# The expert loop's first input slices are copied ahead of the combine weights, and the weights' transposes move into the loop's last turn

## Chip, core and metric

One NeuronCore of a Trainium2 chip runs one program. The metric is the device time of one execution in microseconds, from the hardware profiler; the kernel before was timed three times. The engines are named as in the profile: PE (matmuls; PEld is its weight load), DVE, ACT and POOL (vector, scalar and general work), SP (here it only issues DMAs, in order, and waits on semaphores between them).

## What is computed

One inference step of a decoder layer for a prompt group (272 tokens with the meta tokens) and a sample group (32 tokens), 304 tokens in all: a gated merge of two mixers, then a mixture of 32 experts, of which every token uses two, then a norm. The part that this change touches is the mixture. From the reference:

```python
combine = jnp.sum(jax.nn.one_hot(flat_idx, N_EXPERTS, dtype=jnp.float32) * ew[..., None], axis=1)
y = jnp.zeros_like(xf)
for e in range(N_EXPERTS):
    he = jax.nn.silu(xf @ w_exp_gate[e]) * (xf @ w_exp_up[e])
    y = y + combine[:, e:e + 1] * (he @ w_exp_down[e])
```

All is float32. An expert's weights are three matrices of 1024 x 256 numbers (gate, up, down), 1 MiB each; the 32 experts have 96 of them, 100.7 MB.

## The kernel before

The kernel is written engine by engine: each engine has its own instruction list, and semaphores alone set the order between them.

*Gather.* After the router each of the 608 token copies (304 tokens, two experts each) has a slot, sorted by expert. PE gathers the normed rows into slot order by matmuls with selection matrices `sel` (L1432): 16 results `q` of 304 columns, each evicted by ACT into `xs` (L734, semaphore `gat_done`). An expert reads a window of C = 80 slots of `xs`, starting at an offset that DVE reads from memory: `window` (L1158) copies it into one of two buffers `xw`, which lie over `sel`, so no copy may start before the whole gather is done (L1178). Experts with more than 80 tokens get further items from an overflow table (L1183 to L1201); in this run there are none, but the table is always computed.

*Combine weights.* `weights(t)` (L1125) writes, for each of three token tiles, a tile `wsel` of 608 columns that holds each token's weights at its slots; two buffers, so the third step waits for the first to be used. PE turns it by 128-column blocks in `turn_weights(t)` (L1446: 15 transposes, five for tile 0 within the gather, ten behind it) into PSUM banks 4 to 6. DVE then sums the blocks into `wpair` (L1139 to L1146) and makes the 0/1 matrix `selT` (L1147 to L1151). Both are used only after the expert loop, when the experts' results are scaled and summed back per token. Banks 4 and 5 also take the down results of odd experts, so PE waits for these reads (`wT_done`, L1503) ahead of the first such down pass.

*Expert loop.* A loop of 8 turns with 4 experts each (`EXP_SLOTS` = 4 weight slots), on PE, ACT, DVE and SP. On PE a turn runs `gate_up` of slot s and then `down` of slot s - 1, with the last `down` at the end: gate-and-up 0, gate-and-up 1, down 0, gate-and-up 2, down 1, gate-and-up 3, down 2, down 3. ACT makes the silu of the gate (L742), DVE the product with up (`hidden`, L1162), then the next window, then half of the results' copy (`results`, L1168); ACT copies the other half (L749). DVE's order is that of its list: the weights' reading, then the first two windows, then the overflow table, then the loop.

*Loads.* SP loads the first four experts when their places come free, before the router. The other 28, 84 loads of 1 MiB, are issued in the loop at L387 by `load_expert`: gate, up, down of one expert, each waiting until the slot's former matrix is used (`eg_mm`, `gu_mm`, `dn_mm`, counted by PE). SP's waits are in order: a wait for a down slot holds up the gate and up loads that come after it.

After the loop PE turns the results back (L1528), ACT and DVE scale them by `wpair`, PE sums them with `selT` (L1544), and DVE and ACT do the last norm.

Of the kernel before, what the change touches and what calls it, by code (L numbers as in the profile page):

```python
# [15 lines left out]
P = 128  # L16
# [65 lines left out]
def trunk(nc, a, o):  # L82
    with ExitStack() as ctx:
# [73 lines left out]
        selT = rounded("selT", "work", at_sel + (NT + 2) * SLOTS, PT * T)  # L157
        logit = cut((NG + NE) * NT).rearrange("p (t e) -> p t e", t=NT)
        el, oh1, oh2, rank, inw, rtmp = (cut(NE * NT).rearrange("p (t e) -> p t e", t=NT) for _ in range(6))
        item_at, item_no, item_on = (cut(NE * LEVELS).rearrange("p (e k) -> p e k", e=NE) for _ in range(3))  # L160
        goh, gtmp, gex = (cut(NG * NT).rearrange("p (t e) -> p t e", t=NT) for _ in range(3))
# [5 lines left out]
        over_e, over_at, over_n = (over_i[0:1, at:at + n] for at, n in ((0, MAX_OVER), (MAX_OVER, MAX_OVER), (2 * MAX_OVER, 1)))  # L167
        one_of = wsel_f[:, 0:MAX_OVER * NE * LEVELS].rearrange("p (i n) -> p i n", i=MAX_OVER)
        pick = sb("pick", NT * 10).rearrange("p (k t) -> p k t", k=10)
# [173 lines left out]
        def _(sp):  # L343
# [22 lines left out]

            def load_expert(e, s, used=None):

                for m, (n, used_by) in enumerate((("w_exp_gate", eg_mm), ("w_exp_up", gu_mm))):
                    if used is not None:  # L370
                        sp.wait_ge(used_by, used)
                    sp.dma_start(w_gu_flat[s][m], a[n][0, bass.ds(e, 1)].rearrange("e (p k) f -> p (e k f)", p=P))\
                      .then_inc(gu_in[s], 16)
                if used is not None:
                    sp.wait_ge(dn_mm, used)
                sp.dma_start(w_dn_flat[s], a["w_exp_down"][0, bass.ds(e, 1)].rearrange("e (p k) n -> p (e k n)", p=P))\
                  .then_inc(dn_in[s], 16)

            for b in range(NBLK):
# [414 lines left out]
        def _(dve):  # L794
# [330 lines left out]
            def weights(t):  # L1125

                n, w = ROWS[t], wsel[0:ROWS[t], t % 2]
                if t == NT - 1:
                    dve.wait_ge(wT_used, 1)
                step(vec.tensor_scalar(w, iota[0:n], pos1[0:n, t:t + 1], w1[0:n, t:t + 1], ALU.is_equal, ALU.mult))  # L1130
                step(vec.tensor_scalar(wtmp[0:n], iota[0:n], pos2[0:n, t:t + 1], w2[0:n, t:t + 1],
                                       ALU.is_equal, ALU.mult))
                vec.tensor_tensor(w, w, wtmp[0:n], ALU.add).then_inc(wsel_done, 1)
                dve.wait_ge(wsel_done, t + 1)

            for t in range(NT):
                weights(t)
            dve.wait_ge(wT_used, NT)
            step(vec.memset(wpair_t, 0.0))  # L1139
            for t in range(NT):  # L1140
                for j in range(PT):
                    at, k = weight_block(j, t), min(P, SLOTS - j * P)
                    ins = vec.tensor_reduce(wpair_t[0:k, t, j:j + 1], bank[4 + at // 512][0:k, at % 512:at % 512 + ROWS[t]],
                                            AX_X, ALU.add)
            step(ins)
            vec.tensor_reduce(wpair, wpair_t.rearrange("p t j -> p j t"), AX_X, ALU.add).then_inc(wT_done, 1)  # L1146
            for i in range(3):  # L1147
                for lo, hi, k in wT_parts(i):
                    ins = vec.tensor_scalar(selT[0:k, 512 * i + lo:512 * i + hi], bank[4 + i][0:k, lo:hi],
                                            0.0, None, ALU.is_gt)  # L1150
                ins.then_inc(wT_done, 1)  # L1151

# [29 lines left out]

            for k in range(LEVELS):  # L1183
                step.beside(vec.tensor_scalar(item_on[:, :, k], over, float(C * k), None, ALU.is_gt))
                ins = vec.tensor_scalar(item_at[:, :, k], off[:, NE:], float(C * k), None, ALU.add)
                step.beside(ins) if k < LEVELS - 1 else step(ins)
            flat = lambda ap: ap.rearrange("p e k -> p (e k)")
            each = lambda ap: flat(ap).unsqueeze(1).broadcast_to([P, MAX_OVER, NE * LEVELS])
            step(vec.tensor_tensor_scan(flat(item_no), ones_b[:, 0:NE * LEVELS], flat(item_on), 0.0, ALU.mult, ALU.add))
            step(vec.tensor_scalar(table_f[:, 2 * MAX_OVER:], flat(item_no)[:, NE * LEVELS - 1:], 1.0, None, ALU.add))  # L1190
            step(vec.tensor_tensor(item_no, item_no, item_on, ALU.mult))
            numbers = iota[:, 0:MAX_OVER].unsqueeze(2).broadcast_to([P, MAX_OVER, NE * LEVELS])
            step(vec.tensor_tensor(one_of, each(item_no), numbers, ALU.is_equal))
            step(vec.tensor_tensor(one_of, one_of, each(item_at), ALU.mult))
            step(vec.tensor_reduce(table_f[:, MAX_OVER:2 * MAX_OVER], one_of, AX_X, ALU.add))
            step(vec.tensor_copy(item_at, epri.unsqueeze(2).broadcast_to([P, NE, LEVELS])))
            step(vec.tensor_tensor(one_of, each(item_no), numbers, ALU.is_equal))
            step(vec.tensor_tensor(one_of, one_of, each(item_at), ALU.mult))
            step(vec.tensor_reduce(table_f[:, 0:MAX_OVER], one_of, AX_X, ALU.add))
            step(vec.tensor_scalar(table_f[:, 0:MAX_OVER], table_f[:, 0:MAX_OVER], -1.0, float(NE), ALU.mult, ALU.add))  # L1200
            vec.tensor_copy(over_i, table_f).then_inc(over_done, 1)  # L1201
# [46 lines left out]
        def _(pe):  # L1248
# [197 lines left out]
            def turn_weights(t):  # L1446

                if t == 1:
                    pe.wait_ge(gat_done, 2 * KT)
                    pe.wait_ge(tail_done, 1)  # L1450
                if t < NT - 1:
                    pe.wait_ge(wsel_done, t + 1)
                for j in range(PT):
                    if t == NT - 2 and j == PT - 1:
                        pe.wait_ge(wsel_done, NT)
                    w = min(P, SLOTS - j * P)
                    at = weight_block(j, t)
                    ins = tp(bank[4 + at // 512][0:w, at % 512:at % 512 + ROWS[t]],
                             wsel[0:ROWS[t], t % 2, j * P:j * P + w], ident[0:ROWS[t], 0:ROWS[t]])
# [109 lines left out]
```

## Time and profile before

| | |
|---|---|
| three runs | 657.80, 657.99, 660.57 us |
| median | 657.99 us |
| profiled execution | 659.74 us, of which the span of its instructions is 658.0 us |
| mean granted PE clock | 0.951 of full |
| PE busy | 603.7 us (92%), 8135 matmuls |
| DVE busy | 345.8 us (53%) |
| ACT busy | 185.8 us (28%) |
| DMA | 145.08 MB, mean 220 GB/s |
| expert loop | PE from 395.75 to 625.11 us |

The profile is one execution: a page with totals, and views of its trace that answer questions on a stretch, a line or an engine. Times in a view run from the span's start. "Busy" is time in instructions; a matmul's end is modelled, so a busy PE need not be at its peak. Every fp32 matmul of the expert loop shows as two records, so a gate-and-up pass (64 in the code) is 128 records and a down pass 64; the text counts records. "Issue" as the reason of a wait means that the profile shows nothing that the engine waited for.

### The profile page before, as it was taken

The numbers are of one execution on the slowest core, as the hardware profiler recorded it, in microseconds if no ns is written. First come the engines' busy times: TensorE is split into PE (matmuls) and PEld (weight loads), VectorE is DVE, ScalarE is ACT, GpSimd is POOL, SyncE is SP. The second block draws the span as 40 slices with busy tenths as digits, with TensorE's granted clock in tenths as the row PEclk, the third lists the DMA queues.
The fourth block names the chain that finished last, engine by engine and source line by source line (L and its number), as shares of the span: only waits on it lengthen the run. The fifth ranks groups of instructions, "written<-read, shape, count | busy, mean of one in ns | idle before, by whom it ended". The sixth has DMA issues, their size and how long they took to land.

```text
span 658.0 us, 18646 instructions
## 1 busy us (share of the span) xinstructions
PE 603.7 (92%) x8135; PEld 533.7 (81%) x8135; DVE 345.8 (53%) x689; ACT 185.8 (28%) x308; POOL 83.4 (13%) x95
## 2 busy tenths in 40 slices
PE   5999999879798999999998969899999999998993
PEld 5577777657598989997768849899999999998972
DVE  1149996889899999965127736112121111111135
ACT  3121112544573433743025230011021110111033
POOL 1011110307279610041000000000000000000000
PEclk9599999989989999999967898999999999999998
DMA  9793343231325253414076004999999999999402
GB/s 252 242 251 135 125 136 137 113 127 55 129 83 201 80 204 132 166 44 192 0 307 267 1 1 136 390 414 421 421 421 421 422 422 422 421 421 422 206 2 72
DMA packets 41752, 145.08 MB, mean 220 GB/s; under 512 B 6958, under 2 KB 10262, under 8 KB 29414
## 3 DMA queue, kind: packets, MB, share of 16 engines
q1 hardware_dynamic: 33424, 140.88, 55.1%
q10 hardware_dynamic: 8294, 3.73, 2.4%
q8 instruction: 23, 0.38, 0.2%
q14 instruction: 11, 0.09, 0.0%
HBM read 143.02 MB, written 2.43 MB: 221 GB/s over the span
## 4 chain that ended last, share of the span: by engine, by line
PE 39%; DMA 13%; DVE 8%; issue 2%; ACT 1%; SPq 0%; DVEq 0%; ACTq 0%
PE bank L1480 14%; DMA ring<-w_exp_up 13%; PE bank L1494 7%; PE bank L1382 5%; PE bank L1312 4%; PE bank L1432 3%; PE bank L1544 2%; PE bank L1254 1%; DVE w_lo L940 1%; PE bank L1397 1%; PE bank L1409 1%; DVE conv L983 1%; PE bank L1528 1%; DVE half L1055 1%; ACT work L787 1%
## 5 line engine op out<-in xcount | busy, mean ns | idle before, releaser
L1480 PE MATMUL bank<-work,ring 128*64 128x80 f32 x4096 | 149.3, 234 | 14.6 <-DMA ring<-w_exp_up 8.5
L1480 PEld LDWEIGHTS bank<-work,ring 128*64 128x64 f32 x4096 | 146.1, 140 | 16.3 <-issue 11.6
L1317 PE MATMUL bank<-work,ring 128*128 128x304 f32 x512 | 137.1, 429 | 0.9 <-ACT work L539 0.9
L1317 PEld LDWEIGHTS bank<-work,ring 128*128 128x128 f32 x512 | 99.8, 195 | 36.4 <-issue 3.9
L871 DVE SCALAR_TENSOR_TENSOR bank<-work,par,bank 128x272 f32<-128x272 f32 x232 | 96.4, 498 | 0.0
L1165 DVE TENSOR_TENSOR windows<-bank,outst 128x160 f32<-128x160 f32 x32 | 10.4, 324 | 136.2 <-ACT outst L742 135.4
L1494 PE MATMUL bank<-windows,ring 128*64 128x80 f32 x2048 | 76.0, 233 | 2.6 <-issue 2.6
L1494 PEld LDWEIGHTS bank<-windows,ring 128*64 128x64 f32 x2048 | 73.4, 137 | 3.0 <-issue 3.0
L742 ACT ACTIVATE outst<-bank 128x160 f32<-128x160 f32 x32 | 9.7, 303 | 136.9 <-PE bank L1480 136.9
L940 DVE TENSOR_TENSOR w_lo<-ring,w_hi 128x2048 fp32r<-128x2048 f32 x17 | 39.5, 2326 | 15.4 <-ACT w_hi L620 15.4
L1312 PE MATMUL bank<-xn_hi,w_hi 128*128 128x304 f32 x128 | 40.3, 315 | 6.3 <-DVE xn_lo L940 3.3
L620 ACT ACTIVATE w_hi<-ring 128x2048 fp32r<-128x2048 f32 x20 | 38.1, 1909 | 17.6 <-issue 6.4
L1172 DVE COPY work<-bank 128x320 f32 x32 | 15.7, 492 | 47.2 <-PE bank L1494 47.2
L1312 PE MATMUL bank<-xn_lo,w_hi 128*128 128x304 f32 x128 | 39.9, 311 | 0.0
L1312 PE MATMUL bank<-xn_hi,w_lo 128*128 128x304 f32 x128 | 39.7, 310 | 0.0
L457 POOL TENSOR_TENSOR windows<-work,par 128x248 f32<-128x248 f32 x32 | 30.5, 984 | 25.0 <-DVE work L883 25.0
L749 ACT ACTIVATE work<-bank 128x320 f32 x32 | 14.1, 439 | 65.9 <-PE bank L1494 65.9
L1312 PEld LDWEIGHTS bank<-xn_hi,w_hi 128*128 128x128 f32 x128 | 25.2, 197 | 7.0 <-issue 7.0
L1254 PE MATMUL bank<-ident 128*128 128x128 f32 x184 | 28.5, 329 | 2.2 <-POOL ident L421 1.6
L1254 PEld LDWEIGHTS bank<-ident 128*128 128x128 f32 x184 | 27.6, 242 | 2.5 <-POOL ident L421 1.6
L1312 PEld LDWEIGHTS bank<-xn_lo,w_hi 128*128 128x128 f32 x128 | 25.4, 198 | 0.0
L1312 PEld LDWEIGHTS bank<-xn_hi,w_lo 128*128 128x128 f32 x128 | 25.2, 197 | 0.0
(272 smaller groups left out, 806.6 us busy)
## 6 DMA issues: line engine op xcount, KB each, us to landing
ring<-w_exp_gate SPq DMA_DIRECT2D x32, 1024.0 KB, 16.2
ring<-w_exp_up SPq DMA_DIRECT2D x32, 1024.0 KB, 18.0
ring<-w_exp_down SPq DMA_DIRECT2D x32, 1024.0 KB, 16.0
ring<-w_in SPq DMA_DIRECT2D x11, 2048.0 KB, 8.3
ring<-w_rnn_proj SPq DMA_DIRECT2D x2, 2048.0 KB, 7.7
ring<-w_conv_proj SPq DMA_DIRECT2D x2, 2048.0 KB, 8.4
ring<-w_out SPq DMA_DIRECT2D x2, 2048.0 KB, 8.3
ring<-w_in SPq DMA_DIRECT2D x2, 1024.0 KB, 10.8
```

The source lines that it names most:

```text
L457: ins = nc.gpsimd.tensor_tensor(win4[:, :, t, :], g[:, :, t:t + CW], pcw[:, :, c].unsqueeze(1).broadcast_to([P, NS, CW]), ALU.mult)
L620: nc.scalar.activation(hi, w, ACT.Copy).then_inc(whi_done, 1)
L871: ins = vec.scalar_tensor_tensor(y, glu[:, ch, w:w + TP], pcw[:, w, ch:ch + 1], acc, ALU.mult, ALU.add)
L940: vec.tensor_tensor(part, value, as_f32(high), ALU.subtract).then_inc(lo_sem, 1)
L1172: vec.tensor_copy(ys[:, 4:8, bass.ds(at, C)], bank[3 + 2 * b][:, 0:4 * C].rearrange("p (m n) -> p m n", m=4)).then_inc(ys_dve, 1)
L1254: mm(bank[q][:, 0:P], ident, ident, start=True, stop=True)
L1312: ins = mm(bank[m % 4][:, 0:T], w[:, i, cols], xp[i], start=(i == 0 and j == 0), stop=(i == KT - 1 and j == 2))
L1317: ins = mm(bank[m % 4][:, 0:T], mix_w[b % MIX_SLOTS][:, i, (c % MB) * P:(c % MB + 1) * P], xnT[:, i], start=(i == 0), stop=(i == KT - 1))
L1382: ins = mm(bank[q][0:ROWS[t]], xp[:, c, tok], w[:, i], start=(c == 0 and j == 0), stop=(c == KT - 1 and j == 2))
L1432: ins = mm(bank[q % 4][:, 0:T], part[t][0:n, q // 2 * P:(q // 2 + 1) * P], sel[0:n, t, (q % 2) * T:(q % 2 + 1) * T], start=(t == 0 and par ...
L1480: ins = mm(bank[b][lo:lo + HP, (2 * m + f) * C:(2 * m + f + 1) * C], w_gu[s][m][:, k, f, lo:lo + HP], xw[b][:, k], start=(k == 0), stop=(k ...
L1494: ins = mm(bank[2 + 2 * b + m // 4][lo:lo + HP, (m % 4) * C:(m % 4 + 1) * C], w_dn[s][:, f, m * P + lo:m * P + lo + HP], hid[b][:, f], sta ...
```

## The change

1. DVE's list: the overflow table and the three `weights(t)` steps come first, while the gather runs; then the first two windows; the reading of the turned weights becomes a function `turned_weights` that runs inside the loop, in the last turn, at s = 0 behind the window's copy.
2. `wsel` gets three buffers in place of two, and `one_of`, which lay over it, a place of its own.
3. PE's list: `turn_weights` leaves the gather; all 15 transposes run in the last turn behind the first gate-and-up pass, after waits for the results of expert 27 to be copied out of the banks. The wait for `wT_done` at s = 2 applies in the last turn alone. Both are branches on the turn's number.
4. SP: `load_expert` is split. In the loop the down load of slot s - 1 is issued behind gate and up of slot s; the last down load closes the turn.

```diff
-        wsel_f = cut(2 * SLOTS)
-        wsel = wsel_f.rearrange("p (b n) -> p b n", b=2)
+        wsel = cut(NT * SLOTS).rearrange("p (b n) -> p b n", b=NT)
...
-            def load_expert(e, s, used=None):
+            def load_gate_up(e, s, used=None):
...
+            def load_down(e, s, used=None):
+
                 if used is not None:
                     sp.wait_ge(dn_mm, used)
...
             with sp.Fori(1, NE // EXP_SLOTS) as g:
                 for s in range(EXP_SLOTS):
-                    load_expert(g * EXP_SLOTS + s, s, g * EXP_SLOTS + (s + 1 - EXP_SLOTS))
+                    load_gate_up(g * EXP_SLOTS + s, s, g * EXP_SLOTS + (s + 1 - EXP_SLOTS))
+                    if s:
+                        load_down(g * EXP_SLOTS + (s - 1), s - 1, g * EXP_SLOTS + (s - EXP_SLOTS))
+                s = EXP_SLOTS - 1
+                load_down(g * EXP_SLOTS + s, s, g * EXP_SLOTS + (s + 1 - EXP_SLOTS))
...
             def weights(t):
 
-                n, w = ROWS[t], wsel[0:ROWS[t], t % 2]
-                if t == NT - 1:
-                    dve.wait_ge(wT_used, 1)
+                n, w = ROWS[t], wsel[0:ROWS[t], t]
...
+            for t in range(NT):
+                weights(t)
+            def turned_weights():
+
+                dve.wait_ge(wT_used, NT)
+                step(vec.memset(wpair_t, 0.0))
...
             with dve.Fori(0, NE // EXP_SLOTS) as g:
                 for s in range(EXP_SLOTS):
                     ahead = offset(g * EXP_SLOTS + (s + 2))
                     hidden(g * EXP_SLOTS + s, s % 2)
                     window(ahead, s % 2)
+                    if s == 0:
+                        with dve.If(g > NE // EXP_SLOTS - 2):
+                            turned_weights()
+                        with dve.Else():
+                            dve.nop()
...
             def turn_weights(t):
 
-                if t == 1:
-                    pe.wait_ge(gat_done, 2 * KT)
-                    pe.wait_ge(tail_done, 1)
-                if t < NT - 1:
-                    pe.wait_ge(wsel_done, t + 1)
+                pe.wait_ge(wsel_done, t + 1)
...
             for q in range(4, 2 * KT):
-                if q == 10:
-                    turn_weights(0)
                 pe.wait_ge(gat_done, q - 3)
...
-            turn_weights(1)
-            turn_weights(2)
...
                     gate_up(g * EXP_SLOTS + s, s, s % 2, g * 32 + 32, g * EXP_SLOTS + (s + 1))
+                    if s == 0:
+                        with pe.If(g > NE // EXP_SLOTS - 2):
+                            pe.wait_ge(ys_act, NE - EXP_SLOTS + RESULTS_BEFORE)
+                            pe.wait_ge(ys_dve, NE - EXP_SLOTS + RESULTS_BEFORE)
+                            for t in range(NT):
+                                turn_weights(t)
+                        with pe.Else():
+                            pe.nop()
                     if s == 2:
-                        pe.wait_ge(wT_done, 4)
+                        with pe.If(g > NE // EXP_SLOTS - 2):
+                            pe.wait_ge(wT_done, 4)
+                        with pe.Else():
+                            pe.nop()
```

The overflow table's lines are unchanged and stand ahead of the `weights` loop.

## Rows read from the trace of the kernel before

**Rows 1.** The page: what the DMA engines moved, in 40 slices of 16.45 us

```profile
GB/s 252 242 251 135 125 136 137 113 127 55 129 83 201 80 204 132 166 44 192 0 307 267 1 1 136 390 414 421 421 421 421 422 422 422 421 421 422 206 2 72
```

**Rows 2.** The chain that ended last, expert loop: start us, us, what

```profile
450.36 4.43 PE bank L1494 x128
...
454.78 8.91 PE bank L1480 x256
...
586.17 4.65 PE bank L1480 x128
...
594.07 21.83 DMA ring<-w_exp_up
...
616.03 4.65 PE bank L1480 x128
...
625.11 0.67 issue
```

**Rows 3.** Waits, 400 to 640: who <- whom: us in total, times, longest

```profile
PE bank L1480 <- DMA ring<-w_exp_up: 8.5, 10, 1.4
...
PE bank L1494 <- issue: 2.6, 2, 1.6
...
PE bank L1480 <- issue: 0.5, 1, 0.5
```

**Rows 4.** Timeline, 368 to 404: start us, us, engine, line, what [idle before]

```profile
370.20 0.60 DVE L1130 TENSOR_SCALAR work<-windows,pick 128x608 f32<-128x608 f32 x1
...
372.30 0.59 DVE L1130 TENSOR_SCALAR work<-windows,pick 128x608 f32<-128x608 f32 x1
...
380.36 0.76 PE L1458 MATMUL bank<-ident,work 128*128 128x128 f32 x5
...
380.88 7.41 PE L1432 MATMUL bank<-sel,half 128*128 128x304 f32 x36
...
388.32 0.51 ACT L734 ACTIVATE work<-bank,par 128x304 f32<-128x304 f32 x1 [0.71 <-PE bank L1432]
...
388.89 1.20 PE L1458 MATMUL bank<-ident,work 128*128 128x128 f32 x10 [0.60 <-ACT work L734]
...
395.13 0.88 DVE L1160 COPY work<-work 128x640 f32 x2
...
395.75 10.37 PE L1480 MATMUL bank<-work,ring 128*64 128x80 f32 x242 [5.67 <-DVE work L1160]
...
403.24 0.17 DVE L1201 CAST over_i<-over_f 128x15 int32<-128x15 f32 x1
```

**Rows 5.** Timeline of SP: start us, us, line, the first reloads issued

```profile
400.10 0.35 SPq L372 DMA_DIRECT2D ring<-w_exp_gate  x1
...
402.16 0.34 SPq L372 DMA_DIRECT2D ring<-w_exp_up  x1
...
409.58 0.33 SPq L376 DMA_DIRECT2D ring<-w_exp_down  x1
```

**Rows 6.** Windows: us, busy of each engine, PE clock, DMA share, GB/s

```profile
390.00:391.00 1.00, 0.09 (x2) 0.00 (x0) 0.74 (x5) 0.14 (x1) 0.00 (x0) 1.00 0.00 0
...
393.00:394.00 1.00, 0.00 (x0) 0.00 (x0) 0.99 (x4) 0.00 (x0) 0.00 (x0) 0.50 0.00 0
...
407.00:412.00 5.00, 5.00 (x150) 5.00 (x148) 1.22 (x3) 0.74 (x2) 0.00 (x0) 1.00 0.29 77
...
426.00:427.00 1.00, 0.00 (x0) 0.00 (x0) 0.00 (x0) 0.00 (x0) 0.00 (x0) 1.00 0.89 320
```

**Rows 7.** Windows of PE alone, first loop turn: us, busy (matmuls), clock, DMA

```profile
395.70:406.40 10.70, 10.37 (x242) 0.83 0.48 173
...
406.40:416.50 10.10, 8.94 (x253) 1.00 0.65 248
...
416.50:427.20 10.70, 9.11 (x253) 1.00 0.99 388
```

More of the change, by code:

```diff
@@ L153, in trunk @@
         sel = rounded("sel", "work", at_sel, NT * SLOTS).rearrange("p (t n) -> p t n", t=NT)
-        wsel_f = cut(2 * SLOTS)
-        wsel = wsel_f.rearrange("p (b n) -> p b n", b=2)
+        wsel = cut(NT * SLOTS).rearrange("p (b n) -> p b n", b=NT)
         cut(PT * T)
-        selT = rounded("selT", "work", at_sel + (NT + 2) * SLOTS, PT * T)
+        selT = rounded("selT", "work", at_sel + 2 * NT * SLOTS, PT * T)
         logit = cut((NG + NE) * NT).rearrange("p (t e) -> p t e", t=NT)
         el, oh1, oh2, rank, inw, rtmp = (cut(NE * NT).rearrange("p (t e) -> p t e", t=NT) for _ in range(6))
+        one_of = cut(MAX_OVER * NE * LEVELS).rearrange("p (i n) -> p i n", i=MAX_OVER)
         item_at, item_no, item_on = (cut(NE * LEVELS).rearrange("p (e k) -> p e k", e=NE) for _ in range(3))
@@ L377, in load_expert @@
                   .then_inc(dn_in[s], 16)
+            def load_expert(e, s, used=None):
+                load_gate_up(e, s, used)
+                load_down(e, s, used)
             for b in range(NBLK):
@@ L1134, in weights @@
                 dve.wait_ge(wsel_done, t + 1)
+            for k in range(LEVELS):
+                step.beside(vec.tensor_scalar(item_on[:, :, k], over, float(C * k), None, ALU.is_gt))
+                ins = vec.tensor_scalar(item_at[:, :, k], off[:, NE:], float(C * k), None, ALU.add)
+                step.beside(ins) if k < LEVELS - 1 else step(ins)
+            flat = lambda ap: ap.rearrange("p e k -> p (e k)")
+            each = lambda ap: flat(ap).unsqueeze(1).broadcast_to([P, MAX_OVER, NE * LEVELS])
@@ new lines, in _ @@
+            step(vec.tensor_tensor_scan(flat(item_no), ones_b[:, 0:NE * LEVELS], flat(item_on), 0.0, ALU.mult, ALU.add))
+            step(vec.tensor_scalar(table_f[:, 2 * MAX_OVER:], flat(item_no)[:, NE * LEVELS - 1:], 1.0, None, ALU.add))
+            step(vec.tensor_tensor(item_no, item_no, item_on, ALU.mult))
+            numbers = iota[:, 0:MAX_OVER].unsqueeze(2).broadcast_to([P, MAX_OVER, NE * LEVELS])
+            step(vec.tensor_tensor(one_of, each(item_no), numbers, ALU.is_equal))
+            step(vec.tensor_tensor(one_of, one_of, each(item_at), ALU.mult))
@@ new lines, in _ @@
+            step(vec.tensor_reduce(table_f[:, MAX_OVER:2 * MAX_OVER], one_of, AX_X, ALU.add))
+            step(vec.tensor_copy(item_at, epri.unsqueeze(2).broadcast_to([P, NE, LEVELS])))
+            step(vec.tensor_tensor(one_of, each(item_no), numbers, ALU.is_equal))
+            step(vec.tensor_tensor(one_of, one_of, each(item_at), ALU.mult))
+            step(vec.tensor_reduce(table_f[:, 0:MAX_OVER], one_of, AX_X, ALU.add))
+            step(vec.tensor_scalar(table_f[:, 0:MAX_OVER], table_f[:, 0:MAX_OVER], -1.0, float(NE), ALU.mult, ALU.add))
@@ L1136, in _ @@
+            vec.tensor_copy(over_i, table_f).then_inc(over_done, 1)
             for t in range(NT):
                 weights(t)
[L1138 to L1151, printed above, removed]
+            def turned_weights():
+                dve.wait_ge(wT_used, NT)
+                step(vec.memset(wpair_t, 0.0))
+                for t in range(NT):
+                    for j in range(PT):
+                        at, k = weight_block(j, t), min(P, SLOTS - j * P)
+                        ins = vec.tensor_reduce(wpair_t[0:k, t, j:j + 1], bank[4 + at // 512][0:k, at % 512:at % 512 + ROWS[t]],
+                                                AX_X, ALU.add)
+                step(ins)
+                vec.tensor_reduce(wpair, wpair_t.rearrange("p t j -> p j t"), AX_X, ALU.add).then_inc(wT_done, 1)
+                for i in range(3):
+                    for lo, hi, k in wT_parts(i):
+                        ins = vec.tensor_scalar(selT[0:k, 512 * i + lo:512 * i + hi], bank[4 + i][0:k, lo:hi],
+                                                0.0, None, ALU.is_gt)
+                    ins.then_inc(wT_done, 1)
@@ L1181, in _ @@
                 window(firsts[b], b)
[L1183 to L1201, printed above, removed]
             with dve.Fori(0, NE // EXP_SLOTS) as g:
@@ L1446, in turn_weights @@
             def turn_weights(t):
-                if t == 1:
-                    pe.wait_ge(gat_done, 2 * KT)
-                    pe.wait_ge(tail_done, 1)
-                if t < NT - 1:
-                    pe.wait_ge(wsel_done, t + 1)
+                pe.wait_ge(wsel_done, t + 1)
                 for j in range(PT):
-                    if t == NT - 2 and j == PT - 1:
-                        pe.wait_ge(wsel_done, NT)
                     w = min(P, SLOTS - j * P)
@@ L1458, in turn_weights @@
                     ins = tp(bank[4 + at // 512][0:w, at % 512:at % 512 + ROWS[t]],
-                             wsel[0:ROWS[t], t % 2, j * P:j * P + w], ident[0:ROWS[t], 0:ROWS[t]])
+                             wsel[0:ROWS[t], t, j * P:j * P + w], ident[0:ROWS[t], 0:ROWS[t]])
                 ins.then_inc(wT_used, 1)
             for q in range(4, 2 * KT):
-                if q == 10:
-                    turn_weights(0)
                 pe.wait_ge(gat_done, q - 3)
```

1 line of the change is left out of this document (removed).

## The prediction

> **What bounds the kernel now.** I read the page's slices first. In the GB/s line [rows 1] slices 27 to 37, some 180 us of the 658, lie at 414 to 422, and the slices ahead of them hold 1, 136 and 390: a stretch that moves nothing, a start that limps, and a plateau. The plateau is the expert loop. Next the chain of waits [rows 2]: one gate-and-up pass starts at 586.17, and the same pass of the next turn starts at 616.03. That is 29.86 us for a turn of four experts, or twelve loads of 1 MiB, so **2.488 us a load** (421 GB/s). PE needs less: 256 matmuls in 8.91 us (two passes), so 4.43 us for gate and up and 2.21 for down, 6.64 per expert against 7.46 from the DMA. The waits view agrees [rows 3]: PE waits ten times for an up load, 8.5 us in all. So the end of the loop is set by when the stream of 84 reloads (experts 4 to 31) starts, by its gaps, and by what PE has still to do after the last loads. The first four experts were loaded much earlier, so the stream starts when PE has used the first gate slice.
>
> The third view is the timeline of the hand-over [rows 4]. ACT's last gather eviction ends at 388.32 + 0.51 = 388.83, and PE's first expert matmul comes only at 395.75, after 5.67 us of waiting for DVE. In between PE turns ten weight blocks (388.89 to 390.09), DVE reduces and copies them, and only at 395.13 does DVE copy the first window. The fourth is the issue of the loads [rows 5]: gate 4 at 400.10, up 4 at 402.16, and then nothing until down 4 at 409.58, because SP waits there for the first down pass while gate and up slots of expert 1 are already free. From 407 to 412 the DMA moves 77 GB/s [rows 6].
>
> **Part 1: windows ahead of the weights.** Five transposes inside the gather go (0.52 us of PE, 380.36 to 380.88 [rows 4]), so the last eviction ends at about 388.31. DVE's copy follows within 0.05 (as PE follows the eviction now, at 388.89) and PE follows the start of the copy by 0.62, as it does now (395.13 to 395.75): PE starts at about **388.98**, 6.77 us sooner. What must be done on DVE by then: the overflow table, which now runs from 396.01 to 403.41 (7.4 us), and three weight steps of 2.1 us each (370.20 to 372.30) [rows 4]. From 370.20 that is over at 383.9, and 4.4 us of the gather are left to cover it. Without that cover it would push PE back one for one. The third weight step no longer waits for a transpose, as it has a buffer of its own. No wait is added for POOL; DVE's wait for the zeroed tail stands as before.
>
> PE also keeps its clock. Now the granted clock is 1.00 in 390 to 391 and 0.50 in 393 to 394, when PE has had no work since 390.09 [rows 6]; the first 64 matmuls (the gate) take 4.35 us, 395.75 to the issue at 400.10 [rows 5]. After the change PE has no work for about 1.2 us, from 387.77 (380.88 + 7.41 - 0.52 [rows 4]). The near row is 426 to 427: a whole us with no matmul, in a stall of 1.6 [rows 3, 6], and a clock of 1.00. So I take full clock: 64 matmuls in 2.21 + 0.16 to drain, and gate 4 is issued at 388.98 + 2.37 = 391.35. **8.75 us sooner than 400.10** (6.77 + 1.98). If the clock fell all the same, 2 of these would be lost.
>
> **Part 2: down loads behind the next gate and up.** SP then waits for slots in the order in which PE frees them (gate and up of an expert, then down of the one before). Queued behind SP's down wait now stand the next gate and up; after the change they go first, and behind the gate wait stands a down that is freed later anyway. The gap falls away: 77 GB/s over 5 us [rows 6] is 4.1 us of lost transfer, and the next trio adds about 0.4 more. PE frees a load every 2.21 us and the DMA takes 2.488, so SP is ahead from the first load on. I take **4.5 us**.
>
> At the end, the order works too. Now up 31 is the 83rd of the 84 reloads and PE runs gate and up, then two downs behind it. Then it is the 82nd, and downs 30 and 31 land (2.49 and 4.98 us later) before PE wants them (4.65 and 6.86 us later). PE's work behind up 31 stays 9.08 us (616.03 to 625.11), but starts one load sooner: **2.49 us**.
>
> **Part 3: the transposes in the last turn.** Added to PE: 15 transposes, 10 of which take 1.20 us now [rows 4], so 1.8. Their wait (results of expert 27 copied out) is met under the 4.4 us gate-and-up pass before them. DVE adds its 5 us (390.09 to 395.13) between the window of expert 30 and the hidden product of 29. Queued behind it stand that product and the copy of result 28; PE asks for the product only after gate-and-up of 29 and of 30 have run, over 9 us after the transposes, so 5 us are covered; so is PE's own wait for the finished weights, which stands ahead of the same down. On PE itself the slack is the DMA's: after gate-and-up 28 the next up lands 4.98 us later, and 4.65 + 1.8 is 1.5 late; the loads are 7.46 apart and PE needs 6.86, so 0.9 of it is left at 30 and 0.3 at 31. I price it at 0.3 if PE is in step with the DMA, 1.8 if PE itself is the bound.
>
> Each turn gets two branches on PE and one on DVE. No row shows one in a loop. The near rows are the loop's own back edge, at no cost (450.36 + 4.43 = 454.79, next pass at 454.78), and the 0.67 us at 625.11 that a load of a register, a branch and the loop's end take together [rows 2]. I take the back edge, as it too is a branch in the stream of matmuls, and keep 0 to 0.67 each. On DVE it hides: products have over 4 us before PE asks.
>
> **The sum**, in times of the profiled execution. From gate 4 to up 31 now: 615.90 (594.07 + 21.83 [rows 2]) - 400.10 = 215.8, of which 83 loads are 206.5, so 9.3 are left: 4.5 of gaps, 4.8 of start and uneven flow, which I keep. Then: 391.35 + 4.8 + 82 x 2.488 (204.0) = 600.15; + 0.13 to the first matmul + 9.08 = 609.4. Check on PE: 388.98 + 31 gate-and-up passes (137.3) + 30 downs (66.3) + stalls of the first turn (3.1 [rows 3]) + 1.8 = 597.5, before 600.15, so the DMA still decides, by only 2.7 us. The first turn's stalls now meet a stream that is just one load ahead, and may open a gap in it: 0 to 1.5, I take 0.5. The loop ends at 609.9 instead of 625.11: -15.2. What follows the loop (about 33 us) is unchanged, so the span goes from 658.0 to 642.8. The profiled run itself took 659.74, 1.75 above the median of the three runs (657.99); the median less 15.2 is **642.8**.
>
> **Rivals.**
> A. *Branches make PE the bound.* Sixteen of them lie ahead of gate-and-up 31. Up to 2.7 / 16 = 0.17 us each they hide; at 0.67 each PE comes to that pass at 597.5 + 10.7 = 608.2, the loop ends 8.9 later at 617.1, -8.0: 650.0. For it: the one branch with a row costs that. Against: the back edge.
> B. *Slower: code that is fetched again in each turn.* In the first turn PE stalls three times for "issue" (0.5, and 2.6 in two [rows 3]), each after about the same number of matmuls: 242, 253, 253 [rows 7]. That looks like code coming in by pieces under a busy DMA. Later turns show no such stall, so the loop's code stays. The change makes the body longer (15 transposes, two branches) and moves its start. If it no longer stays, each of the eight turns pays the 3.1 us: PE ends at 388.98 + 212.5 + 1.8 + 24.8 = 628.1, 3.0 after 625.11: 661.0. It decides against the change from 2.7 us a turn on ((625.11 - 388.98 - 212.5 - 1.8) / 8). The Trainium skill (Runtime: NRT & Kernel Launch, Instruction fetch mechanics) speaks for it: it says that a taken branch to a target outside the small window of code held forces a fetch before the engine goes on. By that rule the back edge would stall already, and here it doesn't, so the row decides against the rule as far as this body goes.
> C. *The order of the loads gives less than it seems*: the stream has no gap but the end stays as it was (engines of the DMA finish unevenly), or the clock falls. One of them lost is 2.0 to 2.5 us: about 645.2.
>
> **Chances.** The forecast 0.68, A 0.15, B 0.07, C 0.10. Below, the 4.8 us of start and uneven flow could shrink by half, since half of it arose while the stream was starting twice: 640.4. Above, A's end is 650.0. Range 640.4 to 650.0; it leaves out B and a little on either side. 0.5% is 3.3 us, about what a measurement can tell from no change here. Faster by more: forecast, A, C, less a little for a dearer A, 0.91; within: 0.04, as B is just at the bound; slower 0.05.
>
> **What would show it.** Right: PE's first expert matmul near 389 and clock 1.00 there; first reload issued near 391.4; no window under 350 GB/s between 394 and 598; the loop's end 2.5 us closer to the last landing. Wrong: "issue" rows on PE after the first turn (B) or after each gate-and-up pass at the turn's start (A); DVE still in its weight steps after 388.3; a clock of 0.50 after 389.

## The result and the profile after

The changed kernel takes **704.33 us** (median of 4 runs, 702.4 to 705.36) against 658.56 us for the kernel before on the same chip (4 runs): a ratio of 1.0677 with a 95% interval of [1.0653, 1.0701]. It is 46 us slower; the forecast was 15 us faster. The profiled execution has a span of 700.7 us against 658.0.

The page of the changed kernel, with the lines that answer to [rows 1] (a slice is 17.5 us here):

```profile
span 700.7 us, 18671 instructions
...
PEclk8699999999999999999689999979997999799998
...
GB/s 259 231 213 224 16 241 121 71 49 121 122 127 128 214 88 187 41 181 0 409 132 0 199 365 403 418 226 376 380 421 230 368 365 422 213 393 281 0 3 67
...
q8 instruction: 50, 0.82, 0.5%
...
PE 53%; issue 8%; DVE 4%; ACT 1%; DVEq 0%; ACTq 0%
...
L1486 PE MATMUL bank<-work,ring 128*64 128x80 f32 x4096 | 160.1, 240 | 41.3 <-issue 39.9
```

The plateau of [rows 1] is broken three times (226, 230, 213 GB/s). In the chain's shares "issue" has 8% and DMA has none: PE sets the end now, not the stream. PE's idle time ahead of the gate-and-up matmuls is 41.3 us, 39.9 of it for "issue". The queue that brings instructions (q8) moved 50 packets; in the kernel before it moved 23 (packets, MB, share of the engines' time):

```profile
q8 instruction: 23, 0.38, 0.2%
```

The waits of PE from 385 to 680, as [rows 3] for before (who <- whom: us in total, times, longest):

```profile
PE bank L1486 <- issue: 39.9, 17, 6.3
PE bank L1500 <- issue: 9.3, 8, 1.9
```

Before, the same lines had 0.5 and 2.6 us, and 8.5 us of waiting for up loads [rows 3], of which nothing is left. The timeline of PE shows where the stalls lie (start us, us, engine, line, what, and in brackets the idle time before it with what ended it):

```profile
387.85 10.18 PE L1486 MATMUL bank<-work,ring 128*64 128x80 f32 x241 [1.33 <-DVE work L1191]
...
455.31 0.53 PE L1486 MATMUL bank<-work,ring 128*64 128x80 f32 x3 [6.14 <-issue]
459.73 9.95 PE L1486 MATMUL bank<-work,ring 128*64 128x80 f32 x238 [3.90 <-issue]
...
494.10 9.01 PE L1486 MATMUL bank<-work,ring 128*64 128x80 f32 x254
...
527.08 0.52 PE L1486 MATMUL bank<-work,ring 128*64 128x80 f32 x3 [6.19 <-issue]
531.78 9.78 PE L1486 MATMUL bank<-work,ring 128*64 128x80 f32 x238 [4.18 <-issue]
...
600.56 0.52 PE L1486 MATMUL bank<-work,ring 128*64 128x80 f32 x3 [6.27 <-issue]
```

Three turns of the loop begin with a stall of over 6 us, run three matmuls and stall again for about 4. Turn 4, at 494.10, has no stall at all. Windows cut at the turns (us, busy time and count for PE, PEld, DVE, ACT and POOL, PE clock, DMA share, GB/s) give the price:

```profile
422.30:449.20 26.90, 26.87 (x776) 26.70 (x772) 4.87 (x12) 4.26 (x9) 0.00 (x0) 1.00 1.01 414
449.20:494.10 44.90, 29.74 (x769) 28.76 (x771) 4.87 (x12) 4.25 (x9) 0.00 (x0) 0.89 0.85 325
494.10:520.90 26.80, 26.79 (x774) 26.62 (x769) 4.86 (x12) 4.25 (x9) 0.00 (x0) 1.00 0.98 398
520.90:565.80 44.90, 29.50 (x760) 28.53 (x762) 4.87 (x12) 4.25 (x9) 0.00 (x0) 0.88 0.83 320
565.80:594.30 28.50, 28.50 (x780) 28.33 (x778) 4.87 (x12) 4.25 (x9) 0.00 (x0) 0.95 0.99 394
594.30:638.40 44.10, 30.51 (x770) 29.54 (x772) 4.87 (x12) 4.25 (x9) 0.00 (x0) 0.88 0.82 316
```

Turns 3, 5 and 7 take 44.9, 44.9 and 44.1 us, turns 2 and 4 take 26.9 and 26.8: **some 18 us more in each of three turns**, 53 in all. About 44 of that are stalls: 49.2 us of "issue" in the loop, less the five of turn 1, which sum to 5.1. The other 9 are PE at a granted clock of 0.88 to 0.89 on average. In turn 3 the clock is 1.00 up to 452.0, into the first stall, 0.50 between 455.3 and 459.7, 0.52 up to 463.0, and 1.00 again behind that. Turn 6 has no stall either, but its first matmuls still run at a lower clock (0.54 from 565.05 to 568), so it takes 28.5 us. DVE and ACT do the same work in the same time in all of these turns.

In 449 to 495, which holds turn 3, the instruction queue moved 9 packets, in 495 to 520 none. 0.82 MB in 50 packets makes 16 KB a packet, and the compiled PE program has 64 bytes an instruction, so a packet is a **piece of 256 instructions**. The stalls have the same spacing: those of turn 5 lie behind 3, 241, 367, 493, 620 and 746 matmul records, the last five 126 or 127 apart. Each record has a weight load beside it, so that is 252 to 254 instructions and a few waits. Turns 3, 5 and 7 fetch the loop's code again, nine pieces each.

### The profile page after: what moved, and what is told of

Its sections match the earlier page's. It is cut to its first block, busy times and chain, and to the rows that moved or that the text cites. A ratio compares the mean times of both kernels' runs of the same rounds, so it can differ in the third digit from the quotient of the medians.

```text
span 700.7 us, 18671 instructions
## 1 busy us (share of the span) xinstructions
PE 611.2 (87%) x8135; PEld 539.5 (77%) x8135; DVE 345.8 (49%) x689; ACT 185.8 (27%) x308; POOL 84.8 (12%) x95
## 4 chain that ended last, share of the span: by engine, by line
PE 53%; issue 8%; DVE 4%; ACT 1%; DVEq 0%; ACTq 0%
PE bank L1486 22%; PE bank L1500 10%; PE bank L1328 7%; PE bank L1398 5%; PE bank L1448 3%; PE bank L1561 2%; PE bank L1270 1%; PE bank L1425 1%; PE bank L1413 1%; DVE conv L994 1%; PE bank L1545 1%; DVE half L1066 1%; ACT work L798 0%; DVE gel_lo L951 0%; DVE x L1259 0%
## 5 line engine op out<-in xcount | busy, mean ns | idle before, releaser
L1486 PE MATMUL bank<-work,ring 128*64 128x80 f32 x4096 | 160.1, 240 | 41.3 <-issue 39.9
L1486 PEld LDWEIGHTS bank<-work,ring 128*64 128x64 f32 x4096 | 155.2, 144 | 44.5 <-issue 44.4
L1333 PE MATMUL bank<-work,ring 128*128 128x304 f32 x512 | 135.5, 425 | 0.9 <-ACT work L550 0.9
L1500 PE MATMUL bank<-windows,ring 128*64 128x80 f32 x2048 | 79.7, 234 | 9.3 <-issue 9.3
L1500 PEld LDWEIGHTS bank<-windows,ring 128*64 128x64 f32 x2048 | 76.0, 138 | 10.6 <-issue 10.6
L1270 PEld LDWEIGHTS bank<-ident 128*128 128x128 f32 x184 | 26.9, 237 | 3.3 <-issue 1.7
```

Of the source, the lines that this page charges most:

```text
L1270: mm(bank[q][:, 0:P], ident, ident, start=True, stop=True)
L1333: ins = mm(bank[m % 4][:, 0:T], mix_w[b % MIX_SLOTS][:, i, (c % MB) * P:(c % MB + 1) * P], xnT[:, i], start=(i == 0), stop=(i == KT - 1))
L1486: ins = mm(bank[b][lo:lo + HP, (2 * m + f) * C:(2 * m + f + 1) * C], w_gu[s][m][:, k, f, lo:lo + HP], xw[b][:, k], start=(k == 0), stop=(k ...
L1500: ins = mm(bank[2 + 2 * b + m // 4][lo:lo + HP, (m % 4) * C:(m % 4 + 1) * C], w_dn[s][:, f, m * P + lo:m * P + lo + HP], hid[b][:, f], sta ...
```

## The experiments

*Two theories.* Theory 1 (the rival B of the prediction): the loop's code is no longer held from turn to turn. What decides could be how many pieces the loop covers. Counted in the compiled program, without its labels, the loop before has 1556 PE instructions. Its first one stands 22 behind the start of a piece, so the loop ends 42 instructions into a 7th piece. The changed loop has 1591, and its first one stands 9 ahead of the end of a piece, since 31 instructions went from in front of it: it ends 46 instructions into an 8th. The stalls bear the count out. By it the ends of pieces fall behind 242, 495 and 748 records of the loop before, which is where [rows 7] has its three stalls (242, and twice 253 more), and behind 3, 241, 367, 493, 620 and 746 records of the changed loop, the very places of turn 5. (Three more ends in the loop before, and one in turn 5 of the changed loop, are passed without a stall.) Theory 2 (rival A and its kin): the new branches and the transposes themselves make PE stall.

The knob is the number of idle-time matmuls at the start of PE's list, four instructions each, far from the loop.

**1. The changed kernel, moved on by 16 instructions**

```diff
-            keep_clock(2, 24)
+            keep_clock(2, 28)
```

> The changed kernel with 4 more of PE's idle-time matmuls at the very start, so that the expert loop's code begins 16 instructions later and lies over 7 of the 256-instruction pieces in which PE's code arrives, as in the kernel before, and not over 8. Theory 'place of the loop': the refetching in turns 3, 5 and 7 (three gaps of some 10 us and about 5 us of smaller ones each) goes away, instruction packets fall from 50 to about 23, and the time is that of the forecast less the clock that fell at the start: 643 to 646 us. Rival 'length' (the body is too long wherever it begins): still about 704. Rival 'branches' (the two conditional jumps on PE cause the refetch): still about 704.

Measured: 648.5 us (4 runs) where the kernel before takes 661.17 on the same chip, ratio **0.9863 [0.9787, 0.9938]**. The profiled execution is the fastest of the four (646.23 us, span 644.5); the median lies 2.5 us above the expected range. All branches and transposes are there, and the stalls of turns 3, 5 and 7 are gone. The page, the waits (385 to 640) and the timeline of PE:

```profile
q8 instruction: 23, 0.38, 0.2%
...
PE bank L1500 <- issue: 2.8, 2, 1.6
PE bank L1486 <- issue: 2.5, 3, 1.2
PE bank L1486 <- DMA ring<-w_exp_up: 2.2, 4, 0.8
...
387.19 8.30 PE L1486 MATMUL bank<-work,ring 128*64 128x80 f32 x233 [1.33 <-DVE work L1191]
...
420.35 9.01 PE L1486 MATMUL bank<-work,ring 128*64 128x80 f32 x254
...
473.47 9.01 PE L1486 MATMUL bank<-work,ring 128*64 128x80 f32 x254
```

From 420.35 to 473.47 two turns take 53.12 us, 26.56 each, which is four times the 6.64 us an expert of [rows 2] (4.43 + 2.21): the branches cost nothing that shows. Theory 2 falls, and this version is quicker than the changed kernel by 56 us and than the kernel before by 1.4%, an interval of 0.6 to 2.1%.

**2. The kernel before, moved back by 32 instructions** (no branch, no transpose moved): its loop now ends at the 10th instruction of an 8th piece.

```diff
-            keep_clock(2, 24)
+            keep_clock(2, 16)
```

> The kernel before with 8 of the 24 idle-time matmuls at the very start taken away: its expert loop, unchanged and without branches, begins 32 instructions earlier, 10 ahead of a piece's end, and so lies over 8 pieces. Theory 'place of the loop': it gets the same refetching, at least some of the 30 us or more in issue gaps after the first turn, and ends at 690 to 705. Rivals 'length' and 'branches': unchanged at 658.

Measured: 705.26 us, ratio **1.0677 [1.0632, 1.0722]**, the loss of the changed kernel without any of the change. The page and PE's waits in the loop:

```profile
q8 instruction: 50, 0.82, 0.5%
...
PE bank L1480 <- issue: 36.4, 10, 7.3
PE bank L1494 <- issue: 11.6, 11, 2.0
```

**3. The kernel before, moved back by 52**, so that the loop ends within the 7th piece again (`keep_clock(2, 11)`).

> The kernel before with 13 of the 24 idle-time matmuls at the start taken away: the loop begins 52 instructions earlier, 30 ahead of a piece's end, but its own end now lies in the piece before, so that it covers 7 pieces again. Theory 'place of the loop', by the number of pieces covered: about 658, no issue gaps after the first turn. If it is the nearness of the loop's first instruction to a piece's end that counts, it is as slow as the one moved back by 32: 690 to 705.

Measured: 664.12 us (8 runs), 1.0064 [1.0041, 1.0088], 23 packets and no stall for "issue" behind the first turn. So it is the place that decides, not the loss of idle-time matmuls. Of the 0.6% left, some 4 us, a longer stall behind the loop makes 2.9; it varies from kernel to kernel. PE's waits in this run (385 to 640):

```profile
PE bank L1254 <- issue: 3.6, 1, 3.6
```

Before, that one is 0.67 [rows 2]; it is 0.6 in run 1, 1.5 in the changed kernel and up to 4.2 in run 5.

**4 and 5. The changed kernel, moved back by 48 and by 56** (`keep_clock(2, 12)` and `keep_clock(2, 10)`). By the count above (1591 instructions) both end in the 7th piece, the first 2 instructions ahead of its end, the second 10 ahead. The expectations were written with a loop some nine instructions longer, and so put the end of the first into an 8th piece.

> The changed kernel with 12 of the 24 idle-time matmuls at the start gone: the loop begins 57 instructions ahead of a piece's end, far from it, and its last jump is the 7th instruction of a further piece, so it covers 8 pieces. By the count of pieces: refetching, 50 packets or so, 695 to 710. By the nearness of the loop's head to a piece's end: none, 645 to 650.

> As the kernel moved back by 48, with two idle-time matmuls (8 instructions) fewer: the loop's last jump is now 2 instructions ahead of the end of the 7th piece, so it covers 7. By the count of pieces: no refetching, about 23 packets, 645 to 650. If the sequencer needs the piece behind the loop as well when the jump is that near, refetching as with 8 pieces.

Measured: 655.49 and 656.27 us, one run each; 23 packets and no stall for "issue" between turn 1 and the loop's end in both. (They are longer than run 1 outside the loop: PE's first expert matmul comes at 394.0 and 392.6, and it stalls 4.1 and 4.2 us behind the loop.) The stalls of their first turns lie where the count has ends of pieces (behind 391, 516 and 643 records in run 4, behind 395, 520 and 647 in run 5). Both agree with the count of pieces. But in both slow kernels so far the loop's head also stood 9 or 10 instructions ahead of the end of a piece, so the head's place could decide as well. Two more runs separate that.

**6. The changed kernel, moved back by 24** (`keep_clock(2, 18)`): by the count, head 33 ahead of the end of a piece, end 22 into the 8th.

> The changed kernel with 6 fewer idle-time matmuls ahead of the gather, so its loop stands 24 instructions earlier: the loop's head is then 30 instructions ahead of the end of a 256-instruction piece and its last jump 27 instructions into the 8th piece. If the number of pieces that the loop covers decides: gaps at the head of turns 3, 5 and 7 as in the changed kernel, some 50 packets of code, span 698 to 704 us. If it is the nearness of the head to the end of a piece that decides (9 or 10 instructions in the two slow kernels, 30 or more in the quick ones): no such gaps, 23 packets, span 644 to 655 us.

Measured: 702.84 us (one run), span 701.1. PE's timeline at the start of turn 3, after the page's line:

```profile
q8 instruction: 50, 0.82, 0.5%
...
458.96 1.32 PE L1486 MATMUL bank<-work,ring 128*64 128x80 f32 x15 [6.65 <-issue]
463.28 10.05 PE L1486 MATMUL bank<-work,ring 128*64 128x80 f32 x238 [3.00 <-issue]
```

The second stall now comes after 15 matmuls in place of 3, that is 24 instructions later, just as the loop was moved: stalls lie at ends of pieces.

**7. The kernel before, moved back by 32 and its loop cut by 16 instructions.** The head stays where it was in run 2; four matmuls of the last down pass of a turn are left out, so the loop ends in the 7th piece.

```diff
-            keep_clock(2, 24)
+            keep_clock(2, 16)
...
-                    for f in range(FT):
+                    for f in range(1 if s == 3 and m >= 6 else FT):
```

> The kernel before, moved back by 32 instructions as in the slow run of it, but with 4 matmuls (16 instructions) left out of the last down pass of each turn, which leaves a part of every fourth expert's result uncomputed: the loop's head stays 10 instructions ahead of the end of a piece and its last jump falls 6 instructions ahead of the end of the 7th piece. If the number of pieces decides: no gaps after the first turn, 23 packets, span 655 to 662 us. If the head's place decides: gaps in turns 3, 5 and 7 as without the shortening, some 50 packets, span 700 to 705 us.

Measured: 663.87 us (one run), span 662.1, where run 2 has 704.4. PE's timeline across the start of turn 3, after the page's line:

```profile
q8 instruction: 23, 0.38, 0.2%
...
447.88 4.32 PE L1494 MATMUL bank<-windows,ring 128*64 128x80 f32 x120
452.03 9.02 PE L1480 MATMUL bank<-work,ring 128*64 128x80 f32 x256
```

Sixteen instructions fewer in a turn take 42 us off the span, of which the matmuls left out are about 2 (120 records in 4.32 us here, 128 in 4.65 where none are left out). All kernels so far, by the count (on five chips, on which the kernel before takes 658.56 to 662.44 us):

| kernel | head | end | packets | time, us |
|---|---|---|---|---|
| before | 22 behind a start | 42 into the 7th | 23 | 658.56 |
| run 1 | 7 behind a start | 62 into the 7th | 23 | 648.5 |
| run 3 | 30 ahead of an end | 10 short of the 7th's end | 23 | 664.12 |
| run 4 | 57 ahead | 2 short of the 7th's end | 23 | 655.49 |
| run 5 | 65 ahead | 10 short of the 7th's end | 23 | 656.27 |
| run 7 | 10 ahead | 6 short of the 7th's end | 23 | 663.87 |
| changed | 9 ahead | 46 into the 8th | 50 | 704.33 |
| run 2 | 10 ahead | 10 into the 8th | 50 | 705.26 |
| run 6 | 33 ahead | 22 into the 8th | 50 | 702.84 |

The number of pieces decides; the head's place does not, and neither does the end's place within its piece (42 into the 7th is held, 46 into the 8th isn't). Between two instructions short of the 7th's end (held) and ten into the 8th (fetched again) the exact edge stays open.

**8. The order of the loads alone**: the kernel before with the new order of SP's list and nothing else.

> The kernel before with the loads' order alone changed (down behind the next gate and up); PE's code is as before. By the forecast's sum: 4.5 us of gap at the start and 2.49 us at the end go, 658 - 7.0 = 651 us. If the gap at the start was not lost time (rival C): about 655.5. If the order is what slowed the changed kernel: over 660.

Measured: 657.57 us (10 runs), ratio 0.9945 [0.9909, 0.998]. From the issue of gate 4 to the end of the last expert matmul the profile has 222.06 us against 225.01 before: **2.9 us**, where the prediction had 4.5 + 2.49.

**9. Run 1 with the old order**, the same question from the other side.

> The changed kernel moved on by 16 instructions, with the loads in the old order (gate, up, down of one expert). By the order alone on the kernel before (2.9 us from the first reload to the end of the loop), the loop takes 3 us more than with the new order: 647 to 651. By the forecast's sum it would be 7 us more: 651 to 655.

Measured: 654.6 us (9 runs), 0.9934 [0.9896, 0.9971]; gate 4 to the end of the last expert matmul takes 226.65 us against 221.91 in run 1: 4.7 us for the order. The total alone would fall into the range of the forecast's sum, but run 1 ran on another chip, and this profile has a slower first gate pass (gate 4 comes 4.22 us after PE's first expert matmul, in run 1 2.63).

**10. The changed kernel with PE kept busy ahead of the loop**: ten matmuls between gather and loop, which also move the loop on.

```diff
+            keep_clock(7, 10)
+
             with pe.Fori(0, NE // EXP_SLOTS) as g:
```

> The changed kernel with 10 idle-time matmuls on PE between the gather and the expert loop, where PE waits 1.3 us for DVE's first window. They move the loop's code on by 40 instructions (7 pieces) and leave PE no pause. If the pause is what lets the clock fall in the changed kernel's profile (0.50 from 387.9 to 391), the first reload comes about 2.6 us after PE's first expert matmul in every profile, not 4.2, and the time is that of the kernel moved on by 16, or up to 1.9 us less: 643 to 648. If the ten matmuls are late for the window, up to 1 us more.

Measured: 650.95 us (4 runs), 0.9872 [0.982, 0.9925], span 646.2: the same as run 1 within the intervals. Gate 4 is issued 2.63 us after PE's first expert matmul, as in run 1 (389.82 - 387.19), so there was no clock to be won over that run. With the pause the clock is open: eight profiles of the changed kernel and its variants have one of the same length. In three of them gate 4 is issued 2.6 us after PE's first expert matmul (runs 1, 4 and 6), in five 4.1 to 4.3 us after it (the changed kernel, runs 5, 9, 11 and 12). One profile with no pause can't show that it would always keep the clock.

**11 and 12. Run 1 with PE delayed once by 7.4 us**, behind the first down pass of turn 1, or of turn 4. The question was why the order brings so much less than forecast. (The expectations took 3.5 us for the 32 matmuls; they took 7.4.)

```diff
+                    if s == 1:
+                        with pe.If(g < 1):
+                            keep_clock(7, 32)
+                        with pe.Else():
+                            pe.nop()
```

(`g == 3` in the other.)

> The changed kernel moved on by 16 instructions, with 32 idle-time matmuls (some 3.5 us) on PE in the loop's first turn, behind the first down pass; the code covers 7 pieces. If a late PE in the first turn starves the reloads (they wait for the slots that PE frees, and the queue is one load deep), the whole stretch from the first reload to the loop's end gets longer by about the delay, from 221.9 to some 225.4 us. If the DMA makes the early gaps by itself, the delay is swallowed there and the stretch grows by under 1.5 us.

> The same kernel with the delay in the fourth turn in place of the first. There the queue holds several loads and PE is ahead of the DMA by 2 to 3 us at the end of the loop, so the stretch from the first reload to the loop's end grows by 0.5 to 1.5 us, less than with the delay in the first turn. If it grows by as much, PE is the bound all the way and the early gaps cost nothing.

Measured: 657.39 us (8 runs), 0.9958 [0.9944, 0.9972], and 660.09 us (8 runs), 0.9984 [0.9954, 1.0014]. By the totals the delay in turn 1 is the cheaper one, but it isn't the same delay: the idle-time matmuls there run while code is still coming in, and turn 1 has only 2.5 us of "issue" left, against 5.3 in run 1. Counted from the issue of gate 4, turn 1 is 4.1 us longer than in run 1 (38.88 - 33.15, less 1.65 that its first gate pass took longer), and the stretch up to the end of the last expert matmul is 3.9 longer (225.79 against 221.91): nearly one for one. With the delay in turn 4, turns 1 and 4 together are 9.4 us longer (1.9 and 7.5) and the stretch 6.0, more than the 0.5 to 1.5 expected of half the delay. The missing 3.5 are what run 1 still had in turns 7 and 8 beyond PE's own work (29.53 + 28.82 against 26.56 + 28.3, the last with the transposes). PE's waits (385 to 690) agree: the delay in turn 1 leaves waits for up loads,

```profile
PE bank L1486 <- DMA ring<-w_exp_up: 2.2, 4, 0.8
PE bank L1500 <- issue: 1.3, 1, 1.3
...
PE bank L1486 <- issue: 1.2, 1, 1.2
```

and the delay in turn 4 leaves none (3.9 us is the stall behind the loop):

```profile
PE bank L1486 <- issue: 4.2, 3, 2.4
PE bank L1270 <- issue: 3.9, 1, 3.9
```

So nearly all the time that PE loses in turn 1 is lost at the end, since it makes the stream later; of time lost in the middle, 3.5 us are covered.

## Why the prediction was wrong

**The step that failed: "Later turns show no such stall, so the loop's code stays."** The row was read rightly for the body of before. But the change moves and lengthens that body, and the prediction carried the row over with a chance of 0.07 for B without working out where the body stands. The page of before (23 packets, 0.38 MB) and [rows 7] allowed it: 242 records up to the first stall are 484 instructions, 490 with the others ahead of it, that is 256 + 234, so the head stands 22 behind the start of a piece. 22 + 1556 is 6.2 pieces. Taking 31 instructions away in front (15 transposes of two each, and one more) puts the head 9 ahead of the end of a piece: 9 instructions, six whole pieces, and the 46 left of 1591 reach into an 8th. What no row of before could tell is how many pieces are held; runs 2, 6 and 7 show that seven are and that eight, by ten instructions or more, are not.

**The price of B was wrong too.** It took the 3.1 us of the first turn [rows 3] for each of eight turns, 25 in all, and came to 3 us over the kernel before. Measured are 17.8 us in each of three turns: 14.7 in stalls and 3.1 at the lower clock. In the first turn a stall at the end of a piece takes 0.2 to 2.4 us in the runs here. The jump back to a piece that is gone costs 6.1 to 6.3 us in the changed kernel (6.6 to 7.3 in runs 2 and 6), and the piece after it 3.0 to 5.0 more. Why only every second turn fetches again isn't shown by any run.

**The rule that was put aside.** The Trainium skill (Runtime: NRT & Kernel Launch, Instruction fetch mechanics) has a taken branch to a target outside the code held stall for a fetch. Run 1 goes back seven times over a loop of 7 pieces without a stall, so the code held is more than the rule's two pages. The same section gives PE a store of 2048 instructions, refilled in blocks of 256: eight blocks. By that figure a loop that covers seven leaves one block for what is fetched ahead, and one that covers eight leaves none; an estimate from that page, and every kernel of the table agrees with it. No run here shows the store itself.

With the code held (run 1) the other steps can be read.

**Part 1, windows ahead of the weights: right.** PE's first expert matmul comes at 387.85 in the changed kernel and 387.19 in run 1 (forecast 388.98), and the idle time ahead of it is 1.33 us in place of 5.67 [rows 4]. DVE's weight steps end 4.6 us ahead of the first window's copy in the changed kernel (forecast 4.4). The clock was not settled by the one row that the prediction used: in run 1 gate 4 is issued 2.63 us after that first matmul, in the changed kernel 4.23. (The forecast had 2.37. No row showed its 0.16 to drain, and run 1 has 2.63 - 2.21 = 0.42.) Windows of both (columns as above):

```profile
388.00:391.00 3.00, 3.00 (x48) 3.00 (x50) 0.11 (x1) 0.37 (x1) 0.00 (x0) 0.50 0.03 5
```

```profile
388.00:391.00 3.00, 3.00 (x94) 3.00 (x92) 0.00 (x0) 0.00 (x0) 0.00 (x0) 1.00 0.12 22
```

The first is the changed kernel, the second run 1. After the same pause the granted clock is 0.50 in the one, the lower of its two levels, and 1.00 in the other; where the prediction said "2 of these would be lost", the first lost 1.6.

**Part 2, the order: right in kind, mis-sized.** 7.0 us forecast, 2.9 and 4.7 measured (runs 8 and 9). The end of the loop came as worked out: in run 1 up 31 lands at 602.52 and the last expert matmul ends at 611.73, 9.21 later, as before (625.11 - 615.90 [rows 2]), with up 31 one load earlier in the stream. The chain of run 1:

```profile
577.51 25.01 DMA ring<-w_exp_up
602.52 0.14 issue
602.65 4.65 PE bank L1486 x128
607.30 4.43 PE bank L1500 x128
611.73 0.63 issue
```

What fell short is the other term, the gap of 4.5 us. Gate 4 to up 31 takes 212.7 us in run 1, 215.8 before: 2.5 of the difference is the one load, 0.6 is all that is left of the gap's 4.5. (Run 8, with PE's code as before, has 212.9.) The reason given was "SP is ahead from the first load on", since PE frees a load each 2.21 us and the DMA takes 2.488. In turn 1 that isn't so: PE stalls five times there (5.3 us) and takes 33.15 us for twelve loads, 2.76 each. SP's timeline in run 1 has the loads come when PE frees a slot, not when the DMA could start one:

```profile
389.82 0.35 SPq L371 DMA_DIRECT2D ring<-w_exp_gate  x1
391.88 0.34 SPq L371 DMA_DIRECT2D ring<-w_exp_up  x1
394.24 0.33 SPq L371 DMA_DIRECT2D ring<-w_exp_gate  x1
397.26 0.33 SPq L371 DMA_DIRECT2D ring<-w_exp_up  x1
399.47 0.33 SPq L378 DMA_DIRECT2D ring<-w_exp_down  x1
403.29 0.33 SPq L371 DMA_DIRECT2D ring<-w_exp_gate  x1
```

Five loads of 2.488 behind 389.82 is 402.26; the sixth is issued at 403.29, 1.0 late. Followed on through the turn the loads at 409.01, 414.24 and 420.6 are late in the same way, by 0.7, 0.3 and 1.4; such delays sum to 3.4 us, and the sum's miss from gate 4 to up 31 is 212.7 - (204.0 + 4.8 + 0.5) = 3.4. So "start and uneven flow" was 4.8 + 0.5 in the forecast and 8.7 measured; run 11 shows that what turn 1 loses is lost at the end. The stalls grew from 3.1 us in three to 5.3 in five. They did so with the order of the loads alone too: run 8, PE's code as before, has five that sum to 5.0, and run 9, the changed kernel with the old order, four with 3.9. It may be that code comes later when the new order keeps the DMA busier, but no run took the DMA's load away alone, so the cause of the growth is open.

**Part 3, transposes and branches: right.** The 15 transposes take 1.74 us (forecast 1.8) in the last turn, PE's next pass follows them at once, and the branches cost nothing that shows (run 1). The 0.67 us at the loop's end, which the prediction used as rival A's price, was no measure of a branch: the same place has 0.6 us in run 1 and 4.2 in run 5, with the same branches. In the changed kernel:

```profile
642.98 1.74 PE L1468 MATMUL bank<-ident,work 128*128 128x128 f32 x15
644.65 4.65 PE L1486 MATMUL bank<-work,ring 128*64 128x80 f32 x128
```

With its loop moved, the change does what it was worked out to do, less the 3.4 us: gate 4 at 389.82 (forecast 391.35), the loop's end at 611.73 (609.9), the span 644.5 (642.8). That is one execution, the fastest of four. By the ratio of the runs the gain is 1.4%, 0.6 to 2.1, where 15.2 us would be 2.3%.

## What to carry to other kernels

Before moving instructions ahead of a hardware loop or adding to its body, count its instructions on the engine and find its place from the first-turn "issue" stalls, which mark the ends of code pieces: here a loop over seven pieces of 256 ran from the held code, and one over eight lost some 18 us in each of turns 3, 5 and 7, whatever the edit was. Check the count against the stalls: a count some nine instructions too long put run 4 on the wrong side of the edge. When an edit comes out slower with "issue" in front of the loop's first matmul in late turns, move the loop by a few instructions before judging the edit. The stream of loads, which starts here with one free slot, took over nearly all the time that PE lost in its first turn (3.9 of 4.1 us in run 11), so price the first turn by its own rows, not by the steady pace.

## What was unexpected of the hardware

- Only turns 3, 5 and 7 fetch again; turns 2, 4, 6 and 8 run without a stall though the loop is the same (9 packets in 449 to 495, none in 495 to 520).
- Moving unrelated code by 32 instructions made the kernel before 6.8% slower (run 2).
- A pause of PE of 1.33 us ahead of the loop left the granted clock at 1.00 in run 1 and at 0.50 in the changed kernel; the first gate pass was slow in five of eight profiles.
- The code behind the loop comes late as well, by 0.6 to 4.2 us of "issue", in kernels that differ in the place of their code.
